# Loading the expert up-projection weights of a mixture layer in two 4 MB transfers an expert instead of four of 2 MB

## The reference, cut to what matters

```python
def clamped_swiglu(hu):
    x_glu = jnp.minimum(hu[..., ::2], 7.0)
    x_lin = jnp.clip(hu[..., 1::2], -7.0, 7.0)
    return x_glu * jax.nn.sigmoid(1.702 * x_glu) * (x_lin + 1.0)

logits = xf @ w_router + b_router
top_val, top_idx = lax.top_k(logits, 4)
top_w = jax.nn.softmax(top_val, axis=-1)
# for every expert e and the tokens that picked it:
hu = x_pad[toks] @ w_up[e] + b_up[e]                   # (n, 1024) @ (1024, 2048)
y  = clamped_swiglu(hu) @ w_down[e] + b_down[e]        # (n, 1024) @ (1024, 1024)
out = out.at[toks].add(y * gate)
```

## Time and profile before

| | |
|---|---|
| runs | 1309.53, 1311.68, 1313.76 us, median 1311.68 |
| profiled execution | 1309.65 us, span 1307.6 us |
| mean granted TensorE clock | 0.967 |
| PE busy | 1124.9 us (86%) |
| HBM read | 463.24 MB |
| w_up loads | 128 of 2048 KB, median 22.2 us to landing |
| w_down loads | 64 of 2048 KB, median 22.3 us to landing |

### The profile page before, as it was taken

The page is one execution under the profiler, slowest core; times in us unless marked ns, Lnnn a source line. Parts: engine busy times, 40 slices in busy tenths (PEclk is TensorE's granted clock), DMA queues, the critical chain, the costliest instruction groups (busy, mean ns, idle before and its releaser), DMA issues.

```text
span 1307.6 us, 20704 instructions
## 1 busy us (share of the span) xinstructions
PE 1124.9 (86%) x7951; PEld 571.7 (44%) x7952; DVE 312.0 (24%) x802; ACT 257.8 (20%) x395; POOL 0.2 (0%) x4
## 2 busy tenths in 40 slices
PE   5899989996999678988998988989988678787685
PEld 3645678844344234434343343443433233433232
DVE  2025555265112110212211121221111111111112
ACT  3025432113111111101112021111121111111112
POOL 0000000000000000000000000000000000000000
PEclk9999999997999989999998999999999899999898
DMA  9932375454689999649999999999999999999996
GB/s 383 410 131 97 158 292 225 162 193 194 258 340 429 428 428 428 260 143 431 426 428 428 430 426 429 429 429 429 428 431 426 430 429 428 430 428 430 427 431 264
DMA packets 34813, 464.86 MB, mean 355 GB/s; under 512 B 5116, under 2 KB 5460, under 8 KB 6358
## 3 DMA queue, kind: packets, MB, share of 16 engines
q1 hardware_dynamic: 32400, 460.46, 84.2%
q10 hardware_dynamic: 2374, 3.84, 0.8%
HBM read 463.24 MB, written 1.05 MB: 355 GB/s over the span
## 4 chain that ended last, share of the span: by engine, by line
PE 57%; DMA 36%; DVE 3%; issue 2%; ACTq 1%; ACT 1%; SPq 0%; DVEq 0%
DMA ring<-in_w_up 28%; PE psum L993 19%; PE psum L601 17%; PE psum L1070 8%; DMA ring<-in_w_down 7%; PE psum L923 4%; PE psum L985 2%; PE psum L1088 2%; PE psum L607 1%; DVE area L1775 1%; PE psum L673 1%; ACTq L1144 1%; PE psum L968 1%; PE psum L867 1%; DMA x_res<-in_x 0%
## 5 line engine op out<-in xcount | busy, mean ns | idle before, releaser
L993 PE MATMUL psum<-ring,area 128*32 128x512 f32 (+2 forms) x2432 | 386.9, 624 | 74.3 <-DMA ring<-in_w_up 74.2
L993 PEld LDWEIGHTS psum<-ring,area 128*32 128x32 f32 (+2 forms) x2432 | 106.8, 121 | 344.7 <-issue 225.7
L1070 PE MATMUL psum<-ring,area 128*32 128x256 f32 (+2 forms) x2080 | 191.3, 419 | 26.2 <-DVE area L1760 14.8
L923 PEld LDWEIGHTS psum<-area 128*128 128x128 f32 x1056 | 127.3, 200 | 31.9 <-issue 31.9
L923 PE MATMUL psum<-area 128*128 128x128 f32 x1056 | 133.9, 287 | 0.3 <-DVE area L1666 0.3
L1070 PEld LDWEIGHTS psum<-ring,area 128*32 128x32 f32 (+2 forms) x2080 | 76.0, 115 | 131.0 <-issue 66.3
L1735 DVE TENSOR_SCALAR area<-psum 128x256 f32<-128x256 f32 x51 | 21.7, 425 | 398.7 <-PE psum L993 398.7
L1288 ACT ACT_TABLE_LOAD x32 | 41.1, 1283 | 316.9 <-PE psum L968 316.9
L1300 ACT ACTIVATE area<-area 128x256 f32<-128x256 f32 x51 | 21.3, 417 | 412.3 <-DVE area L1735 412.3
L601 PE MATMUL psum<-ring,hT 128*128 128x512 f32 (+1 forms) x192 | 77.5, 559 | 0.0
L601 PE MATMUL psum<-hT,ring 128*128 128x256 f32 x320 | 72.8, 387 | 3.1 <-ACT area L1127 3.1
(11 more groups left out here) (201 smaller groups left out, 655.4 us busy)
## 6 DMA issues: line engine op xcount, KB each, us to landing
ring<-in_w_up SPq DMA_DIRECT2D x128, 2048.0 KB, 22.2
ring<-in_w_down SPq DMA_DIRECT2D x64, 2048.0 KB, 22.3
ring<-in_ada_w SPq DMA_DIRECT2D x12, 2048.0 KB, 14.9
ring<-in_w_in SPq DMA_DIRECT2D x10, 2048.0 KB, 11.2
ring<-in_w_out SPq DMA_DIRECT2D x2, 2048.0 KB, 9.9
ring<-in_w_in SPq DMA_DIRECT2D x2, 1024.0 KB, 21.0
ring<-in_w_branch_b SPq DMA_DIRECT2D x1, 2048.0 KB, 9.4
cst<-in_cst ACTq DMA_DIRECT2D x1, 1184.5 KB, 11.7
```

Source lines behind the costliest of these rows:

```text
L923: ins = pe.matmul(ps[banks[i]][:, kk % 4 * P:(kk % 4 + 1) * P], h2[:, tt, kk * P:(kk + 1) * P], S[:, tt, 0:P], start=(tt == 0 and kk % 4 = ...
L993: ins = pe.matmul(ps[b][g * P // G:(g + 1) * P // G, 0:w], XT[:, kk, t0:t0 + P // G], wt[:, c0:c0 + w], start=False, stop=kk == KT - 1, sk ...
L1070: ins = pe.matmul(ps[b][g * M:(g + 1) * M, 0:w], hidT[:, p, q * P + of * M:q * P + (of + 1) * M], down_weights(kk)[:, g * W + d * CW:g * W ...
```

## The change

w_up is laid out in memory as two parts an expert instead of four: a part holds four k-steps, and a partition's share of it is one run of 32 KB. Each part is one load of 4 MB that fills two neighbouring slots (4 and 5, or 0 and 1). SP issues the first when TensorE has finished k-step 3 of the expert before, the second when its up projection is complete. TensorE waits for the first part before k-step 0 and for the second before k-step 4. The down loads, their waits, and all arithmetic stay.

```diff
-        up_pair = [sem(f"up_pair{i}") for i in range(KT // 2)]
+        up_half = [sem(f"up_half{i}") for i in range(2)]
+        def up_place(j):
+            s = (NF + 2 * j) % RING
+            return ring[:, s * KT * CW:(s + 2) * KT * CW]
+
         def up_weights(kk):
-            return slot(NF + kk // 2)[:, kk % 2 * 2 * F:(kk % 2 + 1) * 2 * F]
+            return up_place(kk // 4)[:, kk % 4 * 2 * F:(kk % 4 + 1) * 2 * F]
...
             def up_load(e, j):
                 src = a["w_up"][ds(e, 1), j, :, :]
-                sp.dma_start(slot(NF + j), src.rearrange("e p n -> p (e n)")).then_inc(up_pair[j], 16)
+                sp.dma_start(up_place(j), src.rearrange("e p n -> p (e n)")).then_inc(up_half[j], 16)
...
-            for j in range(KT // 2):
-                sp.wait_ge(*released[names[NF + j - RING]])
+            for j in range(2):
+                for i in range(2):
+                    sp.wait_ge(*released[names[NF + 2 * j + i - RING]])
                 up_load(0, j)
...
-                for j in range(KT // 2):
-                    if j < KT // 2 - 1:
-                        sp.wait_ge(up_used, (KT - 2) * e - (KT - 2) + 2 * j + 2)
+                for j in range(2):
+                    if j == 0:
+                        sp.wait_ge(up_used, (KT - 2) * e - (KT - 2) + KT // 2)
                     else:
                         sp.wait_ge(up_full, MAX_U * e)
                     up_load(number, j)
...
-                    if kk % 2 == 0:
-                        pe.wait_ge(up_pair[kk // 2], 16 * e + 16)
+                    if kk % 4 == 0:
+                        pe.wait_ge(up_half[kk // 4], 16 * e + 16)
...
                 if last < KT:
-                    pe.wait_ge(up_pair[KT // 2 - 1], 16 * e + 16)
                     for u in range(n_u):
...
-    a["w_up"] = inputs["w_up"][0].reshape(E, KT // 2, 2, P, 2 * F).transpose(0, 1, 3, 2, 4).reshape(
-        E, KT // 2, P, 4 * F)
+    a["w_up"] = inputs["w_up"][0].reshape(E, 2, 4, P, 2 * F).transpose(0, 1, 3, 2, 4).reshape(
+        E, 2, P, 8 * F)
```

## The result

The changed kernel takes 1317.07 us in the median of 8 runs (1315.75 to 1321.84), the kernel before 1310.86 us (8 runs, 1308.87 to 1313.76). The ratio is 1.0048, with an interval of 1.0035 to 1.0061: 6.2 us slower. The forecast was 1321, with the sum at 10.7 us. The profiled execution of after took 1317.03 us.

What follows compares the result with a forecast made beforehand. The prediction took the queue of weights as the bound in the experts' part, except in one hole. Its terms, 1.7 + 1.5 + 1.6 + 5.1 + 0.8 = 10.7 us, led to 1321 us, range 1314 to 1329.

Steps and rivals of the forecast that it cites:

- its 12.4 us: Time a 4 MB load was taken to need from issue to landing when the queue is empty; upper end 13.2.
- F: Transfers of w_up in 32 KB runs: rate bounded at 1% either way, 6 us, and taken as 0.
- B: Light experts behind the last up load: later finish and possible low clock, counted at the end of expert 5, 1.5 us.
- E: The last expert, a light one: 0.15 us plus a clock drop of 0 to 2.8, taken together as 0.8 us.
- D: Experts 11, 14, 17 and 20, after heavy experts: first loads land late and open gaps, 5.1 us, between 3.6 and 6.3.
- First loads, experts 1 and 7: Loads of experts 0, 1 and 7 go out later but land before they are wanted: no cost.
- A: Expert 2: its first up load lands later in a stream saturated from there to 527 us, 1.7 us.
- C: Expert 8, the first load behind the hole in the stream: 1.6 us, added to TensorE's lateness.
- Rival 1: Every burst restarts at the low clock: B 2.9, D 6.3, E 2.9, kernel at 1327; chance 0.2.
- The drop: TensorE falling to the low clock behind the last up load of a light expert, costing 0 to 2.8 us.
- Rival 2: Gaps close by themselves: A, C and D shrink to some 3 us, kernel at 1315; chance 0.1.
- Rival 3: Longer runs move up loads faster in the saturated stretch; must give back 10.7 + 4 us to make the kernel faster; chance 0.05.

Runs made afterwards that it cites:

- after_again: The changed kernel run once more, unaltered: 1317.81 us, ratio 1.0041 to the kernel before.
- fours_16k: The changed kernel, but each 4 MB up load moves every partition's part as two 16 KB runs from the old memory layout: 1323.22 us, ratio 1.0064.
- twos_8k: The kernel before with the same 2 MB up loads, but each partition's part in two runs of 8 KB: 1319.66 us, ratio 1.0061.
- keep_busy: The changed kernel with eight more matmul calls on zeros in every light expert before the wait for the second up load: 1448.73 us, ratio 1.1009.

## Why the prediction was right, point by point

- **Direction and mechanism: right.** The stream sets the time, and a later release costs where it leaves a load less than its 12.4 us. The least is 12.1 to 12.3. The forecast of 1321 was 4 us too high. That is F. The others sum to 11.3 against 10.7, with B and E 1.0 and 0.6 us above their forecasts and D 0.9 below; that they cancel so well is luck.
- **First loads, experts 1 and 7:** no cost, as forecast.
- **A (1.7) and C (1.6):** the first up loads of experts 2 and 8 land 12.2 and 12.3 us after issue. Against before that is 1.5 later at expert 2. Expert 8's lands at 603.4 against 598.2, 5.2 later: TensorE's lateness at expert 6 (512.74 - 509.29) is 3.45, another 0.3 is added until the load is issued, and C is 12.3 - 10.8, less than 1.5.
- **B (1.5, between 0.1 and 2.9):** 3.45 less the 0.9 by which d1 of expert 5 was late leaves 2.5. The stand at expert 5 was 4.38 us and not the 6.3 of the forecast. The low clock struck here; half of it was taken. Rival 1 was right on B. From 430 us on, 19 rows of four light k-steps in after wait for a load, and 16 of them are slow, most at 5.34 instead of 3.64; but nearly all of these are paid out of the next wait.
- **D (5.1, between 3.6 and 6.3):** four gaps (the first up load lands 10.89, 10.69, 10.87 and 10.58 us after the load ahead of it, instead of 9.71), 4.2 us in all. The drop I gave half a chance does come at expert 11 (5.34 at 703.27), but the clock is back for the gathers (3.84, where the earlier trace rows had 4.97), so it costs 1.7 and not 2.8, and expert 12 (722.76) starts with the landing of its load and not behind it. Rival 2 falls.
- **E (0.8):** 1.4. From d1's landing to the end of the span it is 14.5 us, against 13.1. Whether the clock drops here is chance: in `after_again` the last four k-steps take 3.64 and the end 12.8 us.
- **F (0, within 6 either way): the term that was mis-sized.** The runs of 32 KB move faster: 9.72 against 9.79 us, some 0.075 us for each of about 54 up loads in the full queue, -4.1 us. The step that failed is the reading of the share of 1.01 in the earlier trace rows as no cost a run. It only says that the engines never stood. Per 2 MB the pace moved by 0.04 us, under the 0.05 that I had named as a sign of being wrong; the sign was set too wide. Rival 3 had the right sign, at a third of the 14 us that it needed. Nothing was saved by having fewer loads: loads of 4 MB in 16 KB runs (`fours_16k`) keep the old pace.
- **Slips in the working:** rival 1 with 4.8 us more comes to 1332, not 1331. The 2.0 us saved "an expert" is meant for each of the two pairs of an expert, as the 128 us of rival 3 have it. Neither changes the forecast.

A to E, with the 0.3 us beside C, give 11.3 us on the profiled executions, F takes 4.1 back: 7.2, the difference of the spans (1314.8 - 1307.6). This holds for these two traces; with the repeated ones the difference is smaller, as said at expert 6. The medians differ by 6.2, because the profile of before was on the fast side (its repetition had a span of 1309.8).

## What to carry to other kernels

Before giving buffers back in larger pieces, list each load's time from issue to landing: every load for which it is less than a larger load needs from an empty queue opens a gap, and a gap in a saturated stream is never made up. A load a little above that mark can open one too, where TensorE itself becomes late (here 12.2 to 13.6 us at experts 11 to 20). Try a late release and a late start apart: here the gaps at the experts after heavy ones needed both, but in time each alone cost nearly as much as the whole change, which gave part of its loss back by long runs. Lay weights out in long runs wherever a load has cover, for that gain comes with every load; but keep small loads behind a gap and at the end.

## What the runs showed of the hardware

- A contiguous run costs its DMA engine about 9 ns beside its bytes, at 8, 16 and 32 KB alike: 4.97, 4.89 and 4.86 us for 2 MB in the full queue (`twos_8k`, before, after).
- A load of 4 MB lands 12.1 to 12.3 us after issue when the queue is empty or nearly so, one of 2 MB after 7.5 to 7.8 from an empty queue.
- TensorE's granted clock fell from 1.00 to 0.50 (2.4 to 1.2 GHz) in the middle of 9.5 us of gapless matmuls of 32 rows on one group of 32 columns (`keep_busy`). It also fell behind stands of 2.4 us and more, though not behind each: 16 of 19 rows of four light k-steps were slow in after. With matmuls of 64 rows on four column groups side by side in the stand, 2 of 14 rows behind them were slow, where 12 of 14 had been.
